# Banded attention: the scores of two heads from 64 rows of the array each, in place of 128 rows with a zero half

## The chip, the cores and the metric

The program runs on one core of a Trainium2 chip. The core has a matrix engine (TensorE, PE in the profile; its weight loads are listed apart as PEld), a vector engine (VectorE, DVE), an activation engine (ScalarE, ACT), a general engine (GpSimd, POOL) and a queue that issues transfers (SyncE, SP). The array of TensorE has 128 rows, one for each partition of its operands, and 128 columns, one for each partition of its result. The metric is the time of one execution in microseconds on the device; the median of several runs counts.

## What is computed

The reference is a stack of layers on 512 tokens of width 1024: one layer pair with feed-forward, mLSTM and windowed attention, then two layers with other mixers. The part that the change touches is the windowed attention: 16 query heads of size 64, 4 key and value heads, each block of 128 queries against the blocks of keys before, at and behind it.

```
def window_attention(x, w_in, sink, w_out):
    p = x @ w_in
    q = p[..., :nq].reshape(B, nb, BLOCK, N_KV_HEADS, GROUP, HEAD_DIM)
...
    s = jnp.einsum('bnqkgd,bnskd->bnkgqs', q, kw).astype(jnp.float32) * (HEAD_DIM ** -0.5)
...
    s = s - slopes[:, :, None, None] * dist
    s = jnp.where(valid[None, :, None, None], s, MASK_VALUE)
    m = jnp.maximum(jnp.max(s, axis=-1, keepdims=True), sink_l)
    pe = jnp.exp(s - m)
    attn = pe / (jnp.sum(pe, axis=-1, keepdims=True) + jnp.exp(sink_l - m))
    o = jnp.einsum('bnkgqs,bnskd->bnqkgd', attn, vw.astype(jnp.float32)).reshape(B, S, nq)
    return o.astype(x.dtype) @ w_out
```

## The kernel before

The program is a row of stages written out by hand for each engine: each stage has one method for each engine, each engine runs its own list of instructions in order, and semaphores, raised by `then_inc` and awaited by `wait_ge`, tie the lists together. Weights come in units of 128 x 1024 (`fetch`), ScalarE rounds a unit to `whi` (L209), VectorE forms the rest `wlo` (L217), and a projection makes three matmuls for each product (L236 to L238, and L349 to L351 in the output projections). Both copies run ahead of TensorE by a fixed number of units (`AHEAD`).

`Window` is the attention stage. Its first part is a projection of 12 units. Units 0 and 1 give the keys, transposed: 128 partitions are two key heads of 64 each. Units 2 and 3 give the values, which TensorE turns (L1097). Units 4 to 11 give the queries, two heads in the 128 partitions of one unit: `self.q[:, x, :]` holds the head that uses the first key head of its pair in partitions 0 to 63, and the one that uses the second in 64 to 127.

The keys lie in `self.kz`, of 128 partitions, two variants `g`, two units and 512 tokens. Variant 0 has the key head of partitions 0 to 63 and zeros below; variant 1 has zeros above and the key head of partitions 64 to 127. ScalarE writes the one half of a unit (L1149), VectorE the other (L1193), and GpSimd writes the zeros (L1243) as soon as the memory of the stage before is free. A score matmul (L1113) takes all 128 partitions of `q` and one variant, and the zeros cancel the other head.

The second part is a loop over 32 blocks, (t, i): the pair of heads t, and in it the four blocks of 128 queries i. Blocks at the ends (i is 0 or 3) see two blocks of keys, 256 columns; the others three, 384 columns. A block goes through these steps:

- scores, PE L1113: two matmuls, one for each head g, into banks 2 (n mod 2) + g;
- bias and maximum, DVE: `ws` (L1212, one for each head), the maximum (L1218), its minimum with the sink (L1220, L1222);
- exponentials, ACT: `wp` (L1166, two, with the sums) and one of the sink (L1168);
- the sum and its reciprocal, DVE (L1227, L1229), and the scaling of `wp`, POOL (L1250);
- transposes, PE L1138: `wp` into banks 4 and 5, and their copy to `wt`, ACT L1182;
- output, PE L1127 (PV in what follows): `wt` with the values; the head g takes columns 64 g to 64 g + 63 of the array;
- behind the fourth block of a pair: `xh` (ACT L1174) and `xl` (DVE L1235), the operand of the output projection.

TensorE's list in turn m is: scores of block m + 1, output of block m - 4, transposes of block m - 3. ScalarE's is: exponentials of block m, `xh` of block m - 4 if it is the fourth, `wt` of block m - 3. DVE's is: bias and maximum of block m, sum and reciprocal of block m - 1, `xl` of block m - 4. A 32-bit matmul appears in the trace as two records, each with its own weight load; a transpose as one. So a block has four records of scores.

Before the first scores TensorE waits for the last queries (`wev`), for DVE's half of the keys (`wkv`), for the values (`wvt`) and for GpSimd's zeros (`wzero`).

Of the kernel before, what the change touches and what calls it, by code (L numbers as in the profile page):

```python
# [7 lines left out]
P = 128  # L8
T = 512
# [1053 lines left out]
class Window:  # L1063
# [4 lines left out]

    def __init__(self, c, u0, before, after, scope):
        self.c, self.u0, self.before, self.after = c, u0, before, after  # L1070

        def sb(name, shape):
            return c.sb("w" + name, shape, F32, scope)

        self.q, self.kz, self.vt = sb("q", [P, 8, T]), sb("k", [P, 2, 2, T]), sb("v", [P, 4, 2 * P])
        self.dist, self.nsink = sb("d", [P, 3 * P]), sb("ns", [P, 16])
        self.sx = [sb(f"s{i}", [P, 2, 3 * P]) for i in range(2)]
        self.pp = [sb(f"p{i}", [P, 2, 3 * P]) for i in range(4)]
        self.pt = [sb(f"t{i}", [P, 2, 3 * P]) for i in range(2)]
        self.small = [sb(f"m{i}", [P, 16]) for i in range(3)]  # L1080
# [5 lines left out]
    def tensor(self, t):  # L1086
# [12 lines left out]
        for p in range(8, 12):  # L1099
            t.wait_ge(*at("wev", p))  # L1100
        t.wait_ge(*at("wkv", 1))
        t.wait_ge(*at("wvt", 1))
        t.wait_ge(*at("wzero", 1))
        n_units = len(self.blocks)
        for m in range(-1, n_units + 4):
            if m + 1 < n_units:
                n = m + 1
                x, i = self.blocks[n]
                j0, j1 = self.near(i)
                if n >= 2:  # L1110
                    t.wait_ge(*at("wbias", n - 2))
                for g in range(2):
                    ins = t.matmul(c.bank(2 * (n % 2) + g)[:, 0:(j1 - j0 + 1) * P], self.q[:, x, i * P:(i + 1) * P],  # L1113
                                   self.kz[:, g, x // 4, j0 * P:(j1 + 1) * P], start=True, stop=True)
                ins.then_inc(*up("wqk", n))
# [25 lines left out]
    def scalar(self, a):  # L1141
        c = self.c
        up, at = c.up, c.at
        for p in range(12):
            c.hi(a, self.u0 + p + AHEAD)
            a.wait_ge(*at("gemm", "unit", self.u0 + p))
            b = c.bank(p % 4)
            if p < 2:
                a.activation(self.kz[0:64, 0, p, :], b[0:64, :], COPY).then_inc(*up("wev", p))  # L1149
            elif p < 4:  # L1150
                a.activation(c.tmp[p % 2], b, COPY).then_inc(*up("wev", p))
            else:
                a.activation(self.q[:, p - 4, :], b, COPY, scale=0.125).then_inc(*up("wev", p))
# [30 lines left out]
    def vector(self, v):  # L1184
# [3 lines left out]
        for p in range(12):  # L1188
            c.lo(v, self.u0 + p + AHEAD)
            if p < 2:  # L1190
                v.wait_ge(*at("gemm", "unit", self.u0 + p))
                v.wait_ge(*at("wev", p))
                v.tensor_copy(self.kz[64:128, 1, p, :], c.bank(p)[64:128, :]).then_inc(*up("wkv", p))  # L1193
            elif p in (5, 6):
                v.wait_ge(*at("wturn", "v", p - 5))
                v.tensor_copy(self.vt[:, :, (p - 5) * P:(p - 4) * P], blocks(c.bank(p - 1))).then_inc(*up("wvt", p - 5))
# [40 lines left out]
    def gpsimd(self, g):  # L1237
        c = self.c
        up, at = c.up, c.at
        g.wait_ge(*at(*self.after))  # L1240
        g.wait_ge(*at(*self.before.pool_end()))
        for k in range(2):
            g.memset(self.kz[64 - 64 * k:128 - 64 * k, k, :, :], 0.0).then_inc(*up("wzero", k))  # L1243
            g.wait_ge(*at("wzero", k))
        for n, (x, i) in enumerate(self.blocks):
# [839 lines left out]
def build(nc, xin, xtin, wst, vec, row, tab, mats_in, out, plan):  # L2085
    with ExitStack() as ctx:
# [5 lines left out]
        for step in plan:  # L2092
# [13 lines left out]
            else:  # L2106
                with ExitStack() as scope:
                    if kind == "mlstm":
                        mixer, ver = Mlstm(c, u, before, scope), "m"
                    elif kind == "window":  # L2110
                        mixer, ver = Window(c, u, before, after, scope), "w"
                    else:
# [216 lines left out]
```

## Time and profile before

| | us |
|---|---|
| median of 3 runs | 3798.38 |
| lowest and highest | 3796.67, 3801.94 |
| the profiled execution | 3797.86 |
| its span, first to last instruction | 3796.0 |
| mean granted clock of TensorE | 0.973 |

Of the span, PE is busy 3587.8 us, DVE 1702.9, ACT 1300.8 and POOL 284.1. The attention loop runs from 1549 to 1647 us of the span. All rows below come from the one profiled execution; times in them are microseconds from the start of its span, mean durations nanoseconds. A matmul's duration includes its passage through the array, so two records that follow each other overlap in the trace, and the distance of their starts is what one costs.

### The profile page before, as it was taken

To read this page: it belongs to the slowest core of one execution; us is meant where nothing else is said; L and a number is where in the kernel's file an instruction comes from. 1 tells how busy PE (TensorE), PEld (TensorE's weight loads), DVE (VectorE), ACT (ScalarE), POOL (GpSimd) and SP (SyncE) were. 2 spreads that over 40 slices of the span, in tenths; PEclk is the share of its full clock that TensorE was granted. 3 is DMA by queue.
4 is the path that set the end of the run, shared out by engine and by line. 5 is a ranking of instruction groups with operands and counts; after the bars stand their busy time and mean duration, and the time that the engine had idled before them with its cause. 6 is when DMAs were issued, how large, how long until landed. Compare 5 with 4: busy or idle time off the path is not lost.

```text
span 3796.0 us, 42550 instructions
## 1 busy us (share of the span) xinstructions
PE 3587.8 (95%) x17294; PEld 2903.9 (76%) x17294; DVE 1702.9 (45%) x2375; ACT 1300.8 (34%) x2112; POOL 284.1 (7%) x342
## 2 busy tenths in 40 slices
PE   8999999899999999989998997899999987899999
PEld 7888756788888888678887875678888875678887
DVE  3334454533343324663334676544333766544332
ACT  3222334322222222532222555333222555333221
POOL 0000001000000001210001121110000221210000
PEclk9999999999999999999999898899999998899999
DMA  4332211233322232112332112002332211003232
GB/s 156 100 100 88 71 34 56 73 100 99 110 81 95 94 117 77 48 45 95 99 100 96 61 62 67 17 28 89 100 100 79 101 59 64 17 28 96 93 105 72
DMA packets 86896, 301.30 MB, mean 79 GB/s; under 512 B 9264, under 2 KB 14128, under 8 KB 86704
## 3 DMA queue, kind: packets, MB, share of 16 engines
q1 hardware_dynamic: 86704, 298.59, 23.8%
q8 instruction: 138, 2.26, 0.3%
q14 instruction: 54, 0.44, 0.0%
HBM read 296.46 MB, written 2.10 MB: 79 GB/s over the span
## 4 chain that ended last, share of the span: by engine, by line
PE 80%; DVE 12%; ACT 4%; issue 3%; POOL 1%; DMA 0%; DVEq 0%; SPq 0%; ACTq 0%; POOLq 0%
PE ps L236 16%; PE ps L237 16%; PE ps L238 16%; PE ps L349 7%; PE ps L350 7%; PE ps L351 7%; PE ps L1947 2%; PE ps L846 1%; PE ps L1919 1%; DVE wlo L217 1%; PE ps L1959 1%; DVE tmp L1812 1%; PE ps L1910 1%; PE ps L1944 1%; DVE rows L1741 1%
## 5 line engine op out<-in xcount | busy, mean ns | idle before, releaser
L236 PE MATMUL ps<-xh,whi 128*128 128x512 f32 (+2 forms) x3128 | 1218.9, 390 | 38.7 <-DVE xl L489 13.0
L237 PE MATMUL ps<-xl,whi 128*128 128x512 f32 (+2 forms) x3128 | 1183.9, 378 | 0.0
L238 PE MATMUL ps<-xh,wlo 128*128 128x512 f32 (+2 forms) x3128 | 1183.3, 378 | 0.0
L217 DVE TENSOR_TENSOR wlo<-raw,whi 128x1024 fp32r<-128x1024 f32 x535 | 660.4, 1256 | 677.2 <-ACT whi L209 676.5
L236 PEld LDWEIGHTS ps<-xh,whi 128*128 128x128 f32 x3128 | 601.2, 192 | 170.9 <-issue 48.8
L209 ACT ACTIVATE whi<-raw 128x1024 fp32r<-128x1024 f32 x535 | 547.7, 1050 | 534.9 <-PE ps L351 527.9
L237 PEld LDWEIGHTS ps<-xl,whi 128*128 128x128 f32 x3128 | 600.9, 192 | 113.9 <-issue 10.6
L238 PEld LDWEIGHTS ps<-xh,wlo 128*128 128x128 f32 x3128 | 600.4, 192 | 108.5
L679 DVE TENSOR_TENSOR tmp<-tmp,ps 128x512 f32<-128x512 f32 x132 | 90.8, 688 | 826.1 <-ACT tmp L664 741.5
L350 PE MATMUL ps<-wlo,hh 128*128 128x512 f32 x1056 | 415.6, 394 | 0.0
L349 PE MATMUL ps<-whi,hh 128*128 128x512 f32 x1056 | 415.3, 393 | 0.0
L351 PE MATMUL ps<-whi,hl 128*128 128x512 f32 x1056 | 410.2, 388 | 0.0
L664 ACT ACTIVATE tmp<-ps 128x512 f32<-128x512 f32 x132 | 78.9, 598 | 901.3 <-PE ps L238 901.3
L349 PEld LDWEIGHTS ps<-whi,hh 128*128 128x128 f32 x1056 | 198.3, 188 | 45.4
L351 PEld LDWEIGHTS ps<-whi,hl 128*128 128x128 f32 x1056 | 198.2, 188 | 44.5
L350 PEld LDWEIGHTS ps<-wlo,hh 128*128 128x128 f32 x1056 | 198.6, 188 | 39.3
L618 POOL TENSOR_SCALAR xr<-xr,st 128x512 f32<-128x512 f32 x18 | 18.8, 1043 | 1575.6 <-DVE xr L463 1575.6
L681 DVE TENSOR_TENSOR hl<-tmp,hh 128x512 fp32r<-128x512 f32 x132 | 91.5, 693 | 92.2 <-ACT hh L666 92.2
L666 ACT ACTIVATE hh<-tmp 128x512 fp32r<-128x512 f32 x132 | 83.5, 632 | 124.1 <-DVE tmp L679 124.1
L349 PE MATMUL ps<-whi,xh 128*128 128x512 f32 x256 | 101.7, 397 | 14.6 <-DVE xl L1038 9.4
L1982 ACT ACTIVATE np<-ps,nsm 128x128 f32<-128x128 f32 (+3 forms) x128 | 66.3, 522 | 118.8 <-DVE nsm L2051 118.8
L350 PE MATMUL ps<-wlo,xh 128*128 128x512 f32 x256 | 100.6, 393 | 0.0
(295 smaller groups left out, 3290.7 us busy)
## 6 DMA issues: line engine op xcount, KB each, us to landing
raw<-in_w SPq DMA_DIRECT2D x535, 512.0 KB, 3.3
rows<-in_row SPq DMA_DIRECT2D x15, 512.0 KB, 4.6
xr<-in_xt SPq DMA_DIRECT2D x2, 1024.0 KB, 7.2
xr<-in_x SPq DMA_DIRECT2D x1, 2048.0 KB, 7.8
ntb<-in_tab SPq DMA_DIRECT2D x2, 832.0 KB, 5.9
htb<-in_tab SPq DMA_DIRECT2D x2, 640.0 KB, 4.1
out<-tmp SPq DMA_DIRECT2D x4, 256.0 KB, 3.0
out<-rows SPq DMA_DIRECT2D x4, 256.0 KB, 2.3
```

Source lines behind the costliest of these rows:

```text
L209: a.activation(self.whi[u % NW][:, :], self.raw[u % NRAW][:, :], COPY).then_inc(*self.up("whi", u))
L217: v.tensor_tensor(self.wlo[u % NW][:, :], self.raw[u % NRAW][:, :], f32(self.whi[u % NW][:, :]), SUB).then_inc(*self.up("wlo", u))
L236: t.matmul(out, wh, xh, start=first, stop=False)
L237: t.matmul(out, wh, xl, start=False, stop=False)
L238: return t.matmul(out, wl, xh, start=False, stop=last)
L349: t.matmul(b, xh[:, k, sl], wh, start=k == 0, stop=False)
L350: t.matmul(b, xh[:, k, sl], wl, start=False, stop=False)
L351: ins = t.matmul(b, xl[:, k, sl], wh, start=False, stop=k == self.k - 1)
L664: a.activation(c.tmp[j % 2], self.bank(j, 0), SILU).then_inc(*c.up("silu", s, j))
L666: a.activation(self.hh[:, j, :], c.tmp[2 + j % 2], COPY).then_inc(*c.up("hh", s, j))
L679: v.tensor_tensor(h, c.tmp[j % 2], self.bank(j, 1), MULT).then_inc(*c.up("gated", s, j))
L681: v.tensor_tensor(self.hl[:, j, :], h, f32(self.hh[:, j, :]), SUB).then_inc(*c.up("hl", s, j))
```

## The change

The variants with zeros go. `self.k` holds the keys of a unit once, two heads in 128 partitions, and ScalarE writes all of it in one copy for each unit. A score matmul takes only the 64 partitions of its head from `q` and from `k`, that is rows 0 to 63 of the array for g = 0 and rows 64 to 127 for g = 1. VectorE's copies, GpSimd's memsets and the waits for both (`wkv`, `wzero`) are gone, as is the argument `after`, which only the memsets used. Banks, columns, order of blocks and all else stay.

```diff
-        self.q, self.kz, self.vt = sb("q", [P, 8, T]), sb("k", [P, 2, 2, T]), sb("v", [P, 4, 2 * P])
+        self.q, self.k, self.vt = sb("q", [P, 8, T]), sb("k", [P, 2, T]), sb("v", [P, 4, 2 * P])
...
-        t.wait_ge(*at("wkv", 1))
         t.wait_ge(*at("wvt", 1))
-        t.wait_ge(*at("wzero", 1))
...
                 for g in range(2):
-                    ins = t.matmul(c.bank(2 * (n % 2) + g)[:, 0:(j1 - j0 + 1) * P], self.q[:, x, i * P:(i + 1) * P],
-                                   self.kz[:, g, x // 4, j0 * P:(j1 + 1) * P], start=True, stop=True)
+                    d = slice(64 * g, 64 * g + 64)
+                    ins = t.matmul(c.bank(2 * (n % 2) + g)[:, 0:(j1 - j0 + 1) * P], self.q[d, x, i * P:(i + 1) * P],
+                                   self.k[d, x // 4, j0 * P:(j1 + 1) * P], start=True, stop=True)
...
             if p < 2:
-                a.activation(self.kz[0:64, 0, p, :], b[0:64, :], COPY).then_inc(*up("wev", p))
+                a.activation(self.k[:, p, :], b, COPY).then_inc(*up("wev", p))
...
-            if p < 2:
-                v.wait_ge(*at("gemm", "unit", self.u0 + p))
-                v.wait_ge(*at("wev", p))
-                v.tensor_copy(self.kz[64:128, 1, p, :], c.bank(p)[64:128, :]).then_inc(*up("wkv", p))
-            elif p in (5, 6):
+            if p in (5, 6):
...
-        g.wait_ge(*at(*self.after))
-        g.wait_ge(*at(*self.before.pool_end()))
-        for k in range(2):
-            g.memset(self.kz[64 - 64 * k:128 - 64 * k, k, :, :], 0.0).then_inc(*up("wzero", k))
-            g.wait_ge(*at("wzero", k))
```

On VectorE the rows of the projection part of the stage stood so before, up to the first bias of the loop (`wk` are the keys, `wv` the values, `wns` the negated sink):

```order
L1187 TENSOR_SCALAR wns<-vc 128x16
L1193 COPY wk<-ps 64x512
L217 TENSOR_TENSOR wlo<-raw,whi 128x1024
L1193 COPY wk<-ps 64x512
L217 TENSOR_TENSOR wlo<-raw,whi 128x1024 x4
L1196 COPY wv<-ps 128x4x128
L217 TENSOR_TENSOR wlo<-raw,whi 128x1024
L1196 COPY wv<-ps 128x4x128
```

and stand so now:

```order
L1186 TENSOR_SCALAR wns<-vc 128x16
L217 TENSOR_TENSOR wlo<-raw,whi 128x1024 x5
L1191 COPY wv<-ps 128x4x128
L217 TENSOR_TENSOR wlo<-raw,whi 128x1024
L1191 COPY wv<-ps 128x4x128
```

Two copies of half a unit of keys are gone between the splits of weights, and nothing else moved. On TensorE the opening of the loop, from the last matmul of the projection on, was before (behind "waits" stand the semaphores of the instruction):

```order
L238 MATMUL ps<-xh,wlo 128x512
L1113 MATMUL ps<-wk,wq 128x256 [waits s_wkv,s_wev,s_wvt,s_wzero]
L1113 MATMUL ps<-wk,wq 128x256
L1113 MATMUL ps<-wk,wq 128x384 x2
L1113 MATMUL ps<-wk,wq 128x384 [waits s_wbias]
L1113 MATMUL ps<-wk,wq 128x384
L1113 MATMUL ps<-wk,wq 128x256 [waits s_wbias]
```

and is now:

```order
L238 MATMUL ps<-xh,wlo 128x512
L1112 MATMUL ps<-wk,wq 128x256 [waits s_wev,s_wvt]
L1112 MATMUL ps<-wk,wq 128x256
L1112 MATMUL ps<-wk,wq 128x384 x2
L1112 MATMUL ps<-wk,wq 128x384 [waits s_wbias]
L1112 MATMUL ps<-wk,wq 128x384
L1112 MATMUL ps<-wk,wq 128x256 [waits s_wbias]
```

The order on TensorE is the same through the whole program; two waits of one instruction are gone, and the score matmuls have half the rows.

## Rows read from the trace of the kernel before

**Rows 1.** The page, part 1: busy us, share of the span, instructions.

```profile
PE 3587.8 (95%) x17294; PEld 2903.9 (76%) x17294; DVE 1702.9 (45%) x2375; ACT 1300.8 (34%) x2112; POOL 284.1 (7%) x342
```

**Rows 2.** Stretches: length, busy PE, PEld, DVE, ACT, POOL, granted clock, DMA, GB/s.

```profile
1549.47:1634.92 85.45, 77.11 (x535) 52.65 (x534) 73.26 (x226) 60.77 (x190) 31.17 (x60) 1.00 0.02 7
1578.93:1590.15 11.22, 10.58 (x78) 7.37 (x77) 9.40 (x31) 8.16 (x26) 4.16 (x8) 1.00 0.01 2
```

**Rows 3.** Waits in 1549.4 to 1634.9: total us, times, longest.

```profile
ACT wp L1166 <- DVE wm L1220: 23.5, 24, 1.9
...
DVE xl L1235 <- ACT xh L1174: 7.8, 6, 1.5
...
PEld ps L1138 <- issue: 4.6, 27, 0.2
...
DVE wlo L217 <- ACT whi L209: 4.2, 1, 4.2
...
ACT wt L1182 <- PE ps L1138: 0.8, 2, 0.4
```

**Rows 4.** Timeline of settled blocks: start, us, instruction, idle before in brackets.

```profile
1575.34 1.03 PE L1113 MATMUL ps<-wk,wq 128*128 128x256 f32 x4
...
1577.13 0.75 DVE L1212 SCALAR_TENSOR_TENSOR ws<-wd,ps 128x256 f32<-128x256 f32 x2
...
1579.93 0.57 ACT L1174 ACTIVATE xh<-ps 128x512 fp32r<-128x512 f32 x1
1580.01 1.46 PE L1113 MATMUL ps<-wk,wq 128*128 128x384 f32 x4
...
1580.53 0.69 DVE L1235 TENSOR_TENSOR xl<-ps,xh 128x512 fp32r<-128x512 f32 x1 [1.26 <-ACT xh L1174]
1581.14 0.74 DVE L1212 SCALAR_TENSOR_TENSOR ws<-wd,ps 128x256 f32<-128x256 f32 x2
```

**Rows 5.** Groups by form in 1547.5 to 1645: busy us, mean ns, idle before.

```profile
L1113 PE MATMUL ps<-wk,wq 128*128 128x384 f32 x64 | 23.5, 490 | 1.0 <-DVE ws L1212 1.0
L1113 PEld LDWEIGHTS ps<-wk,wq 128*128 128x128 f32 x128 | 21.9, 190 | 11.2 <-DVE ws L1212 4.8 <-ACT wq L1153 1.3
...
L1113 PE MATMUL ps<-wk,wq 128*128 128x256 f32 x64 | 16.7, 384 | 2.9 <-DVE ws L1212 1.9 <-ACT wq L1153 0.9
```

**Rows 6.** Timeline: output and transposes of blocks with 384 columns.

```profile
1584.77 1.15 PE L1127 MATMUL ps<-wt,wv 128*64 128x128 f32 x12 [0.61 <-ACT wt L1182]
...
1585.84 0.88 PE L1138 MATMUL ps<-res,wp 128*128 128x128 f32 x6
```

**Rows 7.** Timeline: the opening of the loop.

```profile
1547.67 2.39 PE L1113 MATMUL ps<-wk,wq 128*128 128x256 f32 x8 [0.95 <-ACT wq L1153]
...
1549.47 0.74 DVE L1212 SCALAR_TENSOR_TENSOR ws<-wd,ps 128x256 f32<-128x256 f32 x2
```

**Rows 8.** Timeline: the end of the first period.

```profile
1567.14 0.60 ACT L1182 ACTIVATE wt<-ps 128x512 f32<-128x512 f32 x1 [0.41 <-PE ps L1138]
...
1569.32 0.69 DVE L1235 TENSOR_TENSOR xl<-ps,xh 128x512 fp32r<-128x512 f32 x1 [1.51 <-ACT xh L1174]
```

**Rows 9.** What goes, and beside what: line L1193, a stretch, timelines.

```profile
L1193 DVE COPY wk<-ps x2: 694/694/694, 1489.3 to 1492.0; 64x512 f32<-64x512 f32 x2
...
1487.00:1520.00 33.00, 33.00 (x170) 28.02 (x169) 10.03 (x10) 9.71 (x13) 0.00 (x0) 1.00 0.29 96
...
1469.44 1.95 POOL L1243 MEMSET wk<- 64x1024 f32 x2 [0.51 <-PE ps L351]
...
1469.94 1.27 DVE L485 TENSOR_TENSOR xl<-ps,xh 128x512 fp32r<-128x512 f32 x2
...
1096.81 1.27 DVE L485 TENSOR_TENSOR xl<-ps,xh 128x512 fp32r<-128x512 f32 x2
```

**Rows 10.** Clock: two stretches, as in rows 2, and a timeline row.

```profile
1470.00:1475.00 5.00, 3.64 (x18) 3.67 (x19) 4.54 (x9) 1.04 (x2) 1.33 (x2) 0.67 0.92 311
...
1471.36 0.35 PE L236 MATMUL ps<-xh,whi 128*128 128x256 f32 x1 [1.98 <-DVE xl L485]
...
1640.00:1645.00 5.00, 3.41 (x36) 2.60 (x34) 0.00 (x0) 1.41 (x2) 0.00 (x0) 1.00 0.00 0
```

More of the change, by code:

```diff
@@ L1067, with __init__ @@
     blocks = [(t, i) for t in range(8) for i in range(4)]
-    def __init__(self, c, u0, before, after, scope):
-        self.c, self.u0, self.before, self.after = c, u0, before, after
+    def __init__(self, c, u0, before, scope):
+        self.c, self.u0, self.before = c, u0, before
         def sb(name, shape):
             return c.sb("w" + name, shape, F32, scope)
-        self.q, self.kz, self.vt = sb("q", [P, 8, T]), sb("k", [P, 2, 2, T]), sb("v", [P, 4, 2 * P])
+        self.q, self.k, self.vt = sb("q", [P, 8, T]), sb("k", [P, 2, T]), sb("v", [P, 4, 2 * P])
         self.dist, self.nsink = sb("d", [P, 3 * P]), sb("ns", [P, 16])
@@ L2110, in build @@
                     elif kind == "window":
-                        mixer, ver = Window(c, u, before, after, scope), "w"
+                        mixer, ver = Window(c, u, before, scope), "w"
                     else:
```

## The prediction

> **What bounds the kernel now.** I read the page's busy times first, then the busy times by stretch, the waits of the attention loop, and last the timeline of single blocks. Over the whole program TensorE is busy 95% of the span [rows 1]. That number says little here, because the change touches one stage, the attention loop, and that stage has its own limit. The stretch table shows it. The loop runs from 1549.47 to 1634.92, 85.45 us for 32 blocks. One pass over a pair of heads (four blocks, which I call a period) takes 11.22 us, and in it PE counts 10.58 us busy and DVE 9.40 us [rows 2]. By busy share PE looks like the limit.
>
> The waits say otherwise. In the loop DVE waits for ScalarE's xh, 7.8 us in 6 pieces, and for ScalarE's whi once, and for nothing else: there is no wait of DVE for PE. ScalarE waits 23.5 us for DVE's maximum (L1220) and for PE only twice, 0.8 us in all [rows 3]. So the chain of the loop is bias, maximum, minimum with the sink (DVE), exponentials (ScalarE), once a period the copy to xh (ScalarE), then xl and the next bias (DVE). The timeline shows where the scores stand to it. The pair of score matmuls that starts at 1575.34 has ended by 1576.37, and DVE takes its result at 1577.13, 0.76 us later; at the change of heads ScalarE's xh at 1579.93 releases xl at 1580.53, and the bias follows at 1581.14 without a pause [rows 4]. The scores are always early. In the tail behind 1634.92 there are none, and at the head DVE starts its first bias at 1549.47, when the split of weights ahead of it (L217, which had waited for ScalarE's whi) is through, while the first scores began at 1547.67 [rows 3, 7].
>
> **The change, part by part.**
>
> Score matmuls, L1113: 32 pairs, four records each. A pair with 384 columns lasts 1.46 us from the first start to the last end, the mean record 0.490, so the records start (1.46 - 0.49) / 3 = 0.32 us apart; with 256 columns the pair lasts 1.03 and the record 0.384, so 0.215 apart [rows 4, 5]. A record is not made cheaper by having fewer rows; what can shrink is the distance, since the two heads now sit in different rows of the array and write different banks. In program order the records are A1 A2 B1 B2. The least gain is that nothing overlaps (four distances, as now). The most is that the pair costs two distances. I take three, A2 beside B1, because the nearest row points between: PV (L1127), whose two heads already take different columns, has 12 records in 1.15 us, 0.096 each, where the transposes, which use all columns, have 6 in 0.88, 0.147 each [rows 6]. Three distances free 16 x 0.32 + 16 x 0.215 = 8.6 us of PE over the loop; two would free 17.1 us. **None of this is on the path in a settled period**: PE then waits longer for ScalarE's wt (it already waits 0.61 us before the PV at 1584.77 [rows 6]), and wt stands in ScalarE's queue behind exponentials that wait for DVE. After the scores come early, DVE is next late, and it is late already.
>
> In one place PE was late. In the first period PE had a backlog, ScalarE waited for its transposes (0.41 us at 1567.14), and DVE's xl at 1569.32 waited 1.51 us, where in a settled period it waits 1.26 [rows 4, 8]. The backlog holds one pair of 384 columns, whose saving of 0.32 us covers it. **Gain: 1.51 - 1.26 = 0.25 us, taken as 0.2.** Bounds: 0 and 0.25, since beyond it DVE's own chain is next.
>
> The mode of the array: today the order is scores (full), PV (half the columns), transposes (full), scores (full), so there are two switches a block; from now on transposes to scores is a third. What a switch costs is seen between PV and transposes: PEld stands 4.6 us in 27 pieces on "issue", 0.17 us each [rows 3]. So 32 x 0.17 = 5.4 us of PE time are added, less than the 8.6 freed. On the path this is between 0 and 5.4 us; I take 0, since the new switch lies ahead of the scores, which have 0.76 us of cover [rows 4], and PE's total falls all the same. The Trainium skill, "TensorEngine Tiling (Array Packing)", Key Properties, states that changing the tiling mode drains the engine; the trace's 0.17 us agrees, and the sum by that rule would be at worst the 5.4 us above.
>
> DVE: two copies of 64 x 512, 0.694 us each, at 1489.3 and 1492.0, go [rows 9]. In that stretch PE is busy 33.00 of 33 us and DVE 10.03 [rows 9]: nothing waited for them. ScalarE's two copies now write 128 rows instead of 64, in the same stretch, where ScalarE is busy 9.71 of 33 us. Both taken as 0; without PE's cover the two copies of DVE would be worth their 1.39 us.
>
> GpSimd: two memsets, 1.95 us together, at 1469.44, go. Its next work is in the loop, and DVE's xl beside them took 1.27 us, exactly as at 1096.81, in the passage between the two plain layers, where no memset runs [rows 9]. So they cost nothing by contention either: 0.
>
> Waits: PE's first score matmul loses two of its four semaphores (wkv, wzero). Both were long set. It may start some tens of ns sooner, and is covered: the first two pairs are issued together from 1547.67 to 1550.06 and DVE wants the first at 1549.47 [rows 7]. 0. No wait is added and no DMA changes. The 4 KB per partition that come free shift addresses and nothing else.
>
> Sum: -0.2 us. The profiled execution took 3797.86 us, 1.86 over its span of 3796.0, and stands 0.5 below the median of 3798.38. From 3798.38 the forecast is **3798.2 us**.
>
> **The rivals.**
>
> 1. The pair does not overlap at all, so that the change does not do what it says. Then PE gains nothing and pays the new switches, behind cover: 3798.4. In favour: A1 A2 B1 B2 is a bad order for overlap. The time can't tell this from the forecast.
>
> 2. The switches reach the path. PE, ScalarE and PE again (wt, PV, transposes, wt) go round nearly as tightly as DVE does, so 0.17 us a block may surface now and then: up to +5.4, 3799 to 3803.8.
>
> 3. Faster: PE is the true bound, as its 10.58 of 11.22 us suggests [rows 2]. Then all that is freed counts: 3798.4 - 8.6 = 3789.8, or 3781.3 with two distances. Against it: no wait of DVE for PE in the loop [rows 3].
>
> 4. Slower, in the loads of weights. Each score record has a load of 0.190 us [rows 5], today hidden beside the record before. If loads into half the rows are not hidden, a period has 16 of them, +3.0 us. PE's work in a period is 11.22 - 0.61 = 10.6; it becomes the bound from 0.6 us more, and 13.6 is 2.4 over: x 85.45 / 11.22 = 7.6 periods gives +18, **3817**. Against it: PV's loads into half the columns are hidden (12 records in 1.15 us [rows 6]).
>
> 5. Slower, by the clock. The granted clock was 0.67 on average in 1470 to 1475, where PE had just stood still for 1.98 us [rows 10]; of its two levels, 1.2 and 2.4 GHz, it was at the lower for most of that stretch. The change makes PE idler: before PV and in the opening of the loop its waits grow by a few tenths. Were the clock at 1.2 GHz for the whole loop, PE's work of 10.6 us a period, less the 2 x 0.32 + 2 x 0.215 = 1.07 freed, 9.5, would be 19.1, +7.8 x 7.6 = +60, 3858; a single stretch of 5 us at that level costs at most 2.5. It decides once the low level holds for more than three such stretches. Against it: in 1640 to 1645, with PV and transposes alone and PE busy 3.41 of 5 us, the granted clock is 1.00 [rows 10], and the loop will stay busier than that. The Trainium skill, "TensorE: Matmul & The Clock Gate", Part 4: PE-mode transpose, states that transposes don't count as activity in the same way; that would leave scores and PV alone to hold the clock, with the price just given. The same row speaks against it.
>
> **Chances.** Forecast 0.60; no overlap 0.17; switches partly on the path 0.08. These three are within 0.2% (7.6 us, about what a measurement of this kernel can tell from no change): 0.85. Faster, rival 3: 0.05. Slower: rival 4 0.05, rival 5 0.05, together 0.10. The range is that of the three equal cases with the spread of the runs shown (3796.67 to 3801.94), one stretch of low clock more or less (2.5 us) and the 5.4 us of switches: 3794.0 to 3804.0. It leaves out rivals 3 to 5, 0.15.
>
> **What the profile after would show.** A score pair of 384 columns, 1.46 us now, should last 0.64 + 0.49 = 1.13 us (0.81 with two distances, 1.46 with no overlap), and one of 256 columns 0.81 instead of 1.03. PE's wait for ScalarE's wt should grow. The period should stay 11.22 us, with xl waiting 1.26 us in all periods, the first one too; DVE should still have no wait for PE. A line "DVE <- PE" in the loop, score loads that no longer lie beside matmuls, or a granted clock under 1.00 between 1550 and 1635 would make the prediction wrong; so would a period under 11.2 us, which would mean that PE was in the chain after all.

## The result and the profile after

The changed kernel takes 3805.12 us, median of 20 runs (3791.99 to 3808.82), against 3797.55 us for the kernel before on the same chip (20 runs, 3792.56 to 3801.94). The ratio of the mean times, here as everywhere below, is 1.0018, with a 95% interval of 1.0011 to 1.0024: slower, by about 0.2%, where no change was forecast, and the median is 1.1 us outside the range. The profiled execution took 3803.18 us, with a span of 3801.3, against 3797.86 and 3796.0.

The page of the changed kernel, the span and part 1, against [rows 1]:

```profile
span 3801.3 us, 42541 instructions
...
PE 3584.8 (94%) x17294; PEld 2896.5 (76%) x17294; DVE 1701.2 (45%) x2373; ACT 1301.2 (34%) x2112; POOL 282.5 (7%) x340
```

TensorE is busy 3 us less and the span is 5.3 us longer. So the totals say nothing again. Next comes the timeline of settled blocks of the changed kernel (the columns are as in [rows 4]; PEld rows are loads of weights):

```profile
1619.94 0.30 PEld L1112 LDWEIGHTS ps<-wk,wq 64*128 64x128 f32 x4 [0.17 <-issue]
1619.94 0.70 PE L1112 MATMUL ps<-wk,wq 64*128 64x256 f32 x4
...
1624.43 0.57 ACT L1173 ACTIVATE xh<-ps 128x512 fp32r<-128x512 f32 x1
...
1624.51 0.92 PE L1112 MATMUL ps<-wk,wq 64*128 64x384 f32 x4
1625.04 0.69 DVE L1230 TENSOR_TENSOR xl<-ps,xh 128x512 fp32r<-128x512 f32 x1 [1.27 <-ACT xh L1173]
...
1629.27 0.93 PE L1126 MATMUL ps<-wt,wv 128*64 128x128 f32 x10 [1.42 <-ACT wt L1181]
```

The change does what it says. A pair of 384 columns lasts 0.92 us where it lasted 1.46, and one of 256 columns 0.70 where it lasted 1.03 [rows 4, 5]. The four loads lie beside each other (0.30 us in all), and the new switch ahead of them is the 0.17 us on "issue". And as forecast, the saved time is turned into waiting: TensorE stands 1.42 us for wt before an output of 384 columns, where it stood 0.61 [rows 6], while xl waits 1.27 us as before.

The windows of the changed kernel show where the time goes (columns as in [rows 2]: length, busy time of the engines, granted clock, DMA):

```profile
1547.50:1550.00 2.50, 1.42 (x4) 0.51 (x4) 2.40 (x7) 0.93 (x4) 0.00 (x0) 0.68 0.46 126
1550.00:1560.00 10.00, 7.25 (x30) 3.77 (x29) 9.41 (x31) 6.32 (x25) 4.17 (x8) 0.50 0.06 23
1560.00:1562.50 2.50, 2.50 (x12) 1.15 (x11) 1.56 (x6) 1.73 (x4) 0.94 (x2) 0.59 0.00 0
1578.93:1590.15 11.22, 9.37 (x81) 5.96 (x76) 9.39 (x30) 8.17 (x27) 4.18 (x8) 1.00 0.01 2
1549.47:1634.92 85.45, 70.73 (x539) 43.97 (x536) 72.02 (x224) 60.87 (x190) 31.30 (x60) 0.93 0.02 6
1636.25:1649.41 13.16, 9.49 (x56) 7.10 (x56) 0.92 (x4) 3.30 (x6) 0.94 (x2) 0.61 0.01 1
1650.00:1660.00 10.00, 9.54 (x35) 7.77 (x36) 2.35 (x3) 1.38 (x2) 0.00 (x0) 0.83 0.16 52
```

The third column from the end is the granted clock. A settled period still takes 11.22 us with DVE 9.39 busy, the very numbers of before. But the clock, 1.00 from 1500 to 1696 us before, is at 0.50, the lower of its two levels (1.2 of 2.4 GHz), in all of 1550 to 1560, and again for most of the tail and for a part of the output projection behind it. The trace's record of the granted clock dates these low stretches: 13.7 us from 1548.4, 10.2 us from 1637.2, 3.4 us from 1650.8. The kernel before has none of the three. The runs without a timeline fit this, since each has its mean granted clock on record: 0.969 to 0.971 in 19 of the 20 runs of the changed kernel, and 0.974 in the one that took 3791.99 us; 0.973 or 0.974 in all 35 runs of the kernel before that stand beside the first experiments.

What the low clock does is to be seen in the timeline and in the waits of 1540 to 1650, again of the changed kernel:

```profile
1562.31 1.02 DVE L1207 SCALAR_TENSOR_TENSOR ws<-wd,ps 128x384 f32<-128x384 f32 x2 [0.84 <-PE ps L1112]
...
1639.90 2.03 PE L1126 MATMUL ps<-wt,wv 128*64 128x128 f32 x12 [0.90 <-ACT wt L1181]
1641.86 1.54 PE L1137 MATMUL ps<-res,wp 128*128 128x128 f32 x6
```

```profile
DVE xl L1230 <- ACT xh L1173: 21.8, 8, 12.2
PE ps L1126 <- ACT wt L1181: 15.5, 19, 1.4
ACT wt L1181 <- PE ps L1137: 12.1, 6, 3.6
...
DVE ws L1207 <- PE ps L1112: 0.8, 1, 0.8
```

An output of 12 records takes 2.03 us in place of 1.15, six transposes 1.54 in place of 0.88 [rows 6]. In the tail, where nothing is left for DVE, ScalarE waits up to 3.6 us for the transposes, and the last xl waits 12.2 us, where it waited 8.5. And the line "DVE <- PE", which the prediction named as the mark of its own failure, is there: once, 0.8 us, under the low clock.

To place the loss over the whole program I matched ScalarE's activations of the two traces one by one (both have 1766) and subtracted their times. The table gives that difference in us for several kernels, each time against the trace of before; its columns are places in the program, by the time of before. It is worked out from the traces and is no view of the profile.

```
                372    412   1560   1620   1664   1701   2050   2146   3789
after          -0.8   -1.4   -1.7   -0.4   +4.9   +5.0   +5.0   +5.0   +5.3
changed_again  -0.4   -1.0   -1.1   +0.3   +5.5   +4.2   +4.9   +4.9   +5.8
rows_only      -0.4   -1.0   -1.3   +0.1   +2.5   +2.5   +2.5   +2.5   +2.1
rest_only      +0.4   +0.4   +0.3   +0.3   +0.3   +0.3   +0.3   +0.3   +0.5
same_rows      +0.6   +0.6   -1.5   +4.1   +4.1   +2.8   +3.5   +3.5   +4.7
half_cols      +0.8   +0.8   +1.0   +2.3   +3.9   +2.5   +3.3   +3.3   +4.9
fill           +0.4   +0.4   +0.5   +1.6   +1.5   +1.5   +1.5   +3.1   +4.2
fill_half      -0.7   -1.2   -1.5   -0.4   +1.2   -0.1   +0.6   -8.4   -8.1
fill_open      -0.1   -0.7   -1.1   -0.1   +1.6   +0.2   +1.0   -8.0   -7.9
fill_tail      +0.1   +0.1   +0.1   +1.5   +3.1   +1.7   +2.5   +2.4   +3.8
next_before    +0.2   +0.3   +0.1    0.0    0.0    0.0    0.0   -8.9   -6.7
next_after     -0.1    0.0   -0.1   +1.3   +6.5   +5.1   +5.8   -3.1   -3.3
next_fill      -0.1    0.0   -0.2   +0.4   +0.3   +0.3   +0.3   -8.5   -6.6
```

The changed kernel comes into the attention 1.7 us ahead of before, which has nothing to do with the change (0.8 at the start of the program, 0.6 at a low stretch near 379 that this execution did not have, and the rest in small pieces). From 1560 to 1664 it loses 6.6 us: 1.3 in the opening, and 5.3 in the tail with the first part of the output projection. Behind that only 0.4 us are lost until the end.

### The profile page after: what moved, and what is told of

Its sections match the earlier page's. It is cut to its first block, busy times and chain, and to the rows that moved or that the text cites. A ratio compares the mean times of both kernels' runs of the same rounds, so it can differ in the third digit from the quotient of the medians.

```text
span 3801.3 us, 42541 instructions
## 1 busy us (share of the span) xinstructions
PE 3584.8 (94%) x17294; PEld 2896.5 (76%) x17294; DVE 1701.2 (45%) x2373; ACT 1301.2 (34%) x2112; POOL 282.5 (7%) x340
## 4 chain that ended last, share of the span: by engine, by line
PE 80%; DVE 12%; ACT 4%; issue 3%; POOL 1%; DMA 0%; DVEq 0%; SPq 0%; ACTq 0%; POOLq 0%
PE ps L236 16%; PE ps L238 16%; PE ps L237 16%; PE ps L350 7%; PE ps L349 7%; PE ps L351 7%; PE ps L1937 2%; PE ps L846 1%; PE ps L1909 1%; DVE wlo L217 1%; PE ps L1949 1%; DVE tmp L1802 1%; PE ps L1900 1%; PE ps L1934 1%; DVE xr L435 1%
## 5 line engine op out<-in xcount | busy, mean ns | idle before, releaser
L351 PE MATMUL ps<-whi,xl 128*128 128x512 f32 x256 | 101.2, 395 | 0.0
```

The lines of the kernel that those rows point to most:

```text
L351: ins = t.matmul(b, xl[:, k, sl], wh, start=False, stop=k == self.k - 1)
```

## Experiments

Each kernel is compared with runs of the kernel before on the same chip, whose median was 3797.08 or 3797.11 us each time; n is the number of its own runs. A timeline is one execution of each kernel.

**Which part of the change it is.** rows_only is the kernel before with the one line of the score matmuls changed; the zeros, copies, memsets and waits all stay:

```diff
-                    ins = t.matmul(c.bank(2 * (n % 2) + g)[:, 0:(j1 - j0 + 1) * P], self.q[:, x, i * P:(i + 1) * P],
-                                   self.kz[:, g, x // 4, j0 * P:(j1 + 1) * P], start=True, stop=True)
+                    d = slice(64 * g, 64 * g + 64)
+                    ins = t.matmul(c.bank(2 * (n % 2) + g)[:, 0:(j1 - j0 + 1) * P], self.q[d, x, i * P:(i + 1) * P],
+                                   self.kz[d, g, x // 4, j0 * P:(j1 + 1) * P], start=True, stop=True)
```

> The kernel before with the score matmuls alone changed: they take 64 rows of q and the half of kz that is not zero; memsets, the copies of VectorE and the four waits stay. Theory I (idle): the score pairs take half of TensorE's time, TensorE idles more where the loop opens and where it ends, and the granted clock falls there; then this kernel shows it all: ratio to before about 1.002 (1.001 to 1.0025), clock under 1.00 in the opening (1548 to 1562) and in the tail (1636 to 1655). Theory II (rows): the clock falls because matmuls of 64 rows count for less, overlap or not: the same here. Theory III (the rest): copies, memsets, waits and moved addresses make the difference: ratio 1.000 here, clock 1.00 in both places.

Measured: 3805.11 us (n = 12), ratio 1.0017 [1.0008, 1.0025].

rest_only is the reverse, the changed kernel with 128 rows for its score matmuls (its keys hold no zeros, so it sums the scores of the two heads):

```diff
-                    d = slice(64 * g, 64 * g + 64)
-                    ins = t.matmul(c.bank(2 * (n % 2) + g)[:, 0:(j1 - j0 + 1) * P], self.q[d, x, i * P:(i + 1) * P],
-                                   self.k[d, x // 4, j0 * P:(j1 + 1) * P], start=True, stop=True)
+                    ins = t.matmul(c.bank(2 * (n % 2) + g)[:, 0:(j1 - j0 + 1) * P], self.q[:, x, i * P:(i + 1) * P],
+                                   self.k[:, x // 4, j0 * P:(j1 + 1) * P], start=True, stop=True)
```

> The changed kernel with the score matmuls back at 128 rows, on the keys without zeros, so each score sums two heads (the product of the other head is not masked; the work of TensorE is that of before). Theories I and II: ratio 1.000 (0.9995 to 1.0005), score pairs of 1.46 and 1.03 us, clock 1.00 in the opening and the tail. Theory III: ratio about 1.002, clock falls as in the changed kernel.

Measured: 3797.62 us (n = 11), ratio 1.0000 [0.9992, 1.0009]. The stretch 1550 to 1560 and the tail, of rows_only and then of rest_only:

```profile
1550.00:1560.00 10.00, 7.25 (x30) 3.34 (x27) 9.44 (x31) 6.67 (x26) 3.80 (x8) 0.50 0.09 35
1640.00:1650.00 10.00, 6.29 (x44) 4.90 (x45) 1.20 (x2) 3.28 (x5) 0.00 (x0) 0.78 0.00 0
```

```profile
1550.00:1560.00 10.00, 6.08 (x21) 3.21 (x20) 9.45 (x29) 5.61 (x21) 3.17 (x6) 1.00 0.16 53
1640.00:1650.00 10.00, 6.68 (x53) 5.21 (x52) 1.92 (x2) 2.95 (x4) 0.00 (x0) 1.00 0.05 10
```

What follows: the score matmuls alone make the loss, by the times of the runs. The profiled execution of rows_only, 3800.00 us, is one of its faster ones: it has the 13.7 us at half clock in the opening, but only 6.8 in the tail, and loses 3.7 us from 1560 to 1664 where the changed kernel loses 6.6. How far the tail falls is thus not the same in each execution. The copies, memsets and waits that went are worth nothing, as forecast, and so are the shifted addresses.

**Is it idleness, or the rows?** TensorE works less on the scores and at fewer rows; two kernels separate these. same_rows puts both heads of a pair into rows 0 to 63 (head 2 of each pair is not computed), so that they can't overlap and TensorE works as long as before. half_cols keeps all 128 rows and halves the columns (half of the scores is not computed):

```diff
-                    d = slice(64 * g, 64 * g + 64)
+                    d = slice(0, 64)
```

> The changed kernel with both score matmuls of a pair in rows 0 to 63 (head 0 computed twice, the second head left out): half the rows, but nothing can overlap, so a pair of 384 columns should take about 1.46 us again, not 0.92. Theory I: TensorE is as busy as before, clock 1.00 in the opening and tail, ratio 1.000 (at most 1.0005). Theory II: half the rows count for less, clock falls, ratio 1.001 to 1.0025.

Measured: 3806.98 us (n = 11), ratio 1.0019 [1.0011, 1.0028].

```diff
-                    d = slice(64 * g, 64 * g + 64)
-                    ins = t.matmul(c.bank(2 * (n % 2) + g)[:, 0:(j1 - j0 + 1) * P], self.q[d, x, i * P:(i + 1) * P],
-                                   self.k[d, x // 4, j0 * P:(j1 + 1) * P], start=True, stop=True)
+                    w = (j1 - j0 + 1) * P // 2
+                    ins = t.matmul(c.bank(2 * (n % 2) + g)[:, 0:w], self.q[:, x, i * P:(i + 1) * P],
+                                   self.k[:, x // 4, j0 * P:j0 * P + w], start=True, stop=True)
```

> The changed kernel with score matmuls of all 128 rows but half the columns (half of each block's scores left out and the heads summed): TensorE's time for a pair is that of the changed kernel (about 0.9 us for the long pairs) with full rows. Theory I: the clock falls in the opening and the tail, ratio 1.001 to 1.0025. Theory II: full rows hold the clock, ratio 1.000.

Measured: 3799.40 us (n = 11, 3790.58 to 3802.73), ratio 0.9998 [0.9989, 1.0007]; its runs stand in two groups, five from 3790.6 to 3792.5 with a mean clock of 0.974 or 0.975, and six from 3799.4 to 3802.7 with 0.971 or 0.972, so the median means little. Pair of 384 columns in the settled part, same_rows, then half_cols:

```profile
1606.87 1.55 PE L1112 MATMUL ps<-wk,wq 64*128 64x384 f32 x4
```

```profile
1604.61 0.82 PE L1112 MATMUL ps<-wk,wq 128*128 128x192 f32 x4
```

The stretch 1550 to 1560 of same_rows, and of half_cols:

```profile
1550.00:1560.00 10.00, 8.56 (x25) 4.59 (x24) 9.12 (x30) 6.48 (x26) 4.07 (x8) 0.56 0.08 30
```

```profile
1550.00:1560.00 10.00, 6.60 (x20) 4.89 (x20) 9.48 (x29) 5.48 (x19) 2.40 (x5) 0.56 0.15 53
```

The pair of 384 columns just ahead of the fall, in same_rows, and the same pair in rest_only, where nothing falls:

```profile
1548.75 1.55 PE L1112 MATMUL ps<-wk,wq 64*128 64x384 f32 x4 [0.28 <-DVE ws L1207]
```

```profile
1550.54 1.56 PE L1111 MATMUL ps<-wk,wq 128*128 128x384 f32 x4 [0.28 <-DVE ws L1206]
```

What follows: the plain form of "TensorE is idler, so the clock falls" does not hold. In same_rows TensorE's work and pauses are those of rest_only to 0.1 us until the clock falls, and it falls for 17.1 us from 1551.3, longer than in the changed kernel. Nine of its eleven runs have a mean clock of 0.969 to 0.972, rest_only's all 0.973 or 0.974. Its settled part is denser too (a pair takes 1.55 us against 1.46), and holds 1.00. The opening costs it 5.6 us in the table against 1.3, since its pairs don't overlap and TensorE at half clock is the bound (DVE waits for its scores three times, 5.0 us in all). But half_cols falls as well, for 13.7 us from 1551.3, with all rows in use and less time at work. So in this opening neither all the rows nor the full time at work was enough alone; what decides these runs don't tell. Nor do the two profiles show the larger part of the loss, that of the tail: from 1636 to 1650 the clock is 1.00 in both, and half_cols has only 3.4 us at half clock behind it. The slower runs of same_rows, 3806 to 3808 us at 0.969 or 0.970, may have more; none of them has a timeline.

**Does the clock carry the loss?** If so, extra work for TensorE that nobody reads has to make the kernel faster. The opening is where TensorE has room: of 1550 to 1560 the kernel before fills 6.04 us. fill adds one 128-row matmul of 512 columns behind the scores of blocks 1 to 4, into a bank that is free there, and one of 384 columns behind the transposes of each of the last four blocks, the first of them behind a wait for the last bias, so that its bank is free; fill_half has the same with 64 rows; fill_open and fill_tail have one of the two places alone:

```diff
+        def fill(n, w):
+            t.matmul(c.bank(n)[:, 0:w], self.q[:, 0, 0:P], self.q[:, 1, 0:w], start=True, stop=True)
...
                 ins.then_inc(*up("wqk", n))
+                if 1 <= n <= 4:
+                    fill(4, 512)
...
                 ins.then_inc(*up("wturn", n))
+                if n == n_units - 4:
+                    t.wait_ge(*at("wbias", n_units - 1))
+                if n >= n_units - 4:
+                    fill(0, 384)
```

> The changed kernel with extra matmuls, whose result is written and never read, that use all 128 rows of the array: one of 512 columns behind the scores of each of blocks 1 to 4 in the opening of the attention, and one of 384 columns behind the transposes of each of its last four blocks. Theory R (rows at work hold the clock; half the rows for the scores lets it fall): both fallen stretches, of 13.7 us from 1548.4 and of 10.2 and 3.4 us from 1637.2, were gone or at least much shorter, and the 5.3 to 7 us that they cost come back. By the shared runs of rest_only (3797.6 us), which has the scores at full rows and otherwise the same code, the ratio would be 0.999 to 1.0002. Theory W (the time is lost in the work itself, by TensorE taking longer for the pair or its new switches, and the clock is only a by-product of the execution): the fillers add work of TensorE, 4 x (0.43 or more) and 4 x (0.32 or more) us at the rate of the settled blocks' 384-column scores (1.46 us for a pair of two at full rows), so the ratio stays at 1.0018 or rises to 1.0025. Theory C (the clock falls by the chip's state, whatever stands in the attention): as the changed kernel, 1.0018.

Measured: 3795.57 us (n = 11, 3789.85 to 3802.18), ratio 0.9996 [0.9987, 1.0005].

> As the run before it, but the extra matmuls use rows 0 to 63 of the array alone: the same time at work of TensorE, half the rows. Theory R: they do less or nothing for the clock, so the low stretches stay, the ratio is 1.0015 to 1.0025, and it differs from that of the kernel with full-row fillers by 0.001 or more. A theory of time at work alone (the clock looks at how long TensorE is busy): the low stretches go as with full rows and the ratio is 0.999 to 1.0002.

Measured: 3791.87 us (n = 11), ratio 0.9991 [0.9982, 1.0000].

> The changed kernel with the four full-row fillers of the opening alone. If the account of the profiled pair is right, the opening lost 1.3 us and the tail with the output projection 5.7: the low stretch at 1548 goes and that near 1637 stays, and the ratio is 1.0010 to 1.0016. If the opening carries most of the loss: 1.0005 or less.

Measured: 3790.17 us (n = 10; eight of them from 3789.2 to 3791.1, the others 3795.1 and 3802.6), ratio 0.9985 [0.9976, 0.9994].

> The changed kernel with the four full-row fillers of the last four blocks alone. By the same account the low stretches from 1637 to 1655 go and that of the opening stays: ratio 1.0000 to 1.0006. If the opening carries most of the loss: 1.0012 or more.

Measured: 3800.70 us (n = 10), ratio 1.0009 [1.0000, 1.0018].

The stretch 1550 to 1560 of fill, fill_half, fill_open and fill_tail, in this order:

```profile
1550.00:1560.00 10.00, 7.33 (x28) 2.60 (x26) 9.45 (x30) 5.49 (x22) 2.98 (x6) 1.00 0.16 53
```

```profile
1550.00:1560.00 10.00, 6.83 (x35) 3.58 (x34) 9.45 (x30) 6.51 (x26) 4.04 (x8) 0.94 0.07 27
```

```profile
1550.00:1560.00 10.00, 7.30 (x36) 3.42 (x34) 9.41 (x32) 6.61 (x25) 3.66 (x7) 0.96 0.11 42
```

```profile
1550.00:1560.00 10.00, 6.90 (x22) 2.83 (x24) 9.45 (x28) 5.65 (x21) 3.22 (x6) 0.52 0.15 52
```

What follows: the fillers of the opening lift the clock in the opening, and those of the tail don't lift it there. With them one low stretch of 3.4 us is left there, which begins at 1558.9 to 1561.0; without them it lasts 13.7. In the tail, fill has no low stretch at all; fill_open and fill_half have 3.4 us near 1648, fill_tail 3.4 from 1649.4, all of them less than the 10.2 and 3.4 of the changed kernel. So most of the tail comes right by itself once the opening does: fill_open, whose tail has the very code of the changed kernel, loses 1.6 us from 1620 to 1664 where that loses 5.3. The tail's fillers do as much by themselves: fill_tail leaves the opening as it is and loses 1.6 as well. Why the tail falls at all, when its work is the same in both, stays open. fill_half does not bear out the expectation that half rows do nothing: as extra work on top they do about what full rows do. That is against a rule by rows alone, as half_cols was.

Three more expectations did not come out. By the account of the profile fill_open was to be at 1.0010 or more, and it is faster than before; 1.0005 or less was named for an opening that carries most of the loss, which its profile doesn't show. fill_tail, at 1.0009, lies between its two branches. half_cols has the ratio of full rows that hold the clock, and a clock that falls. And fill, which has the cleaner attention, is slower than fill_open. The table shows why. fill_open leaves the attention 1.6 us behind before (2.7 lost on the way), and then gains 9.0 us between 2050 and 2146, in another stage, in which no code differs. The window 2090 to 2110 of before, and of fill_open:

```profile
2090.00:2100.00 10.00, 8.69 (x48) 8.69 (x48) 5.59 (x26) 4.78 (x11) 0.00 (x0) 0.64 0.15 52
2100.00:2110.00 10.00, 10.00 (x48) 10.00 (x48) 1.22 (x1) 2.83 (x3) 0.00 (x0) 0.50 0.07 13
```

```profile
2090.00:2100.00 10.00, 7.81 (x70) 7.74 (x70) 6.53 (x30) 5.73 (x15) 0.00 (x0) 1.00 0.17 54
2100.00:2110.00 10.00, 10.00 (x60) 8.78 (x60) 6.21 (x8) 8.65 (x12) 0.23 (x1) 1.00 0.32 105
```

Before has a low stretch of 20.5 us from 2092.9, in dense work of TensorE, and fill_open has none. It is a second place where the clock decides, and it comes and goes between executions. The groups of times fit it: between the two groups of half_cols the mean clock differs by about 0.003, which over 3800 us is some 20 us more or less at half clock (an estimate, from rounded clocks). As long as it does so, a small difference in the attention is read through it.

**The second place held still.** Just ahead of it TensorE of the kernel before waits 2.51 us for VectorE's xl:

```profile
2091.31 0.33 PE L236 MATMUL ps<-xh,whi 128*128 128x128 f32 x1 [2.51 <-DVE xl L489]
```

I filled this wait, in the kernel before (next_before) and in the changed one (next_after), and in a third kernel (next_fill) together with fillers behind the scores of blocks 1 to 6 in the opening of the attention (those behind 5 and 6 into bank 7). changed_again is the changed kernel once more.

```diff
                 self.turn_t(t, 2 + m, h)
+        if self.then is not None:
+            for _ in range(16):
+                t.matmul(banks[1][:, 2 * P:], c.w(u0, 0)[0], c.xh[:, 0, 0:2 * P], start=True, stop=True)
         for i in (2, 3):
```

> The kernel before with 16 extra matmuls of 256 columns (about 0.12 us each, result never read) in one wait of the stage behind the attention: ahead of the first 128-column matmuls of its projection, where TensorE waits 2.51 us at 2091.31 for xl, and behind which the profiled run of before shows the low clock for 20.5 us from 2093. The attention is untouched. Theory P (that stretch is the clock's answer to the 2.51 us wait, and worth 8 to 9 us wherever it comes): low stretch gone, 1.00 from 2090 to 2120, ratio 0.9975 to 0.9980 in nearly all executions, as in the two profiled runs in which it was absent (offsets of 9.0 us between 2090 and 2160). Theory Q (that stretch depends on something else): ratio 1.000.

Measured: 3790.55 us (n = 11, 3788.74 to 3791.91), ratio 0.9982 [0.9973, 0.9991].

> The changed kernel with the same 16 extra matmuls in the stage behind the attention and nothing else. Against before: if the loss of the change is made within the attention and its output projection alone, the median is that of the run before it plus 5 to 8 us (ratio 0.9990 to 1.0000); if half or more of the 7.6 us between the medians of before and after came from how often the later stretch falls, it is within 3 us of it (0.9975 to 0.9985).

Measured: 3793.43 us (n = 11, 3789.28 to 3796.42), ratio 0.9988 [0.9979, 0.9997].

> The changed kernel with those 16 matmuls and with six full-row fillers in the opening of the attention (behind the scores of blocks 1 to 6 in place of 1 to 4). Theory R (clock): the attention's opening costs nothing or at most the 1.1 us of the earlier run, the low stretch at 2093 is gone, and the median is 3786 to 3790 us, ratio 0.9970 to 0.9980, faster than both kernels and at or below the kernel before with the same 16 matmuls. If extra matmuls cost what they save: at or above that kernel.

Measured: 3790.94 us (n = 11, 3788.92 to 3792.64), ratio 0.9983 [0.9974, 0.9992].

> The changed kernel once more, for a second profile. If the low stretches belong to the change and not to the one execution, they stand again in the opening (from about 1548, some 14 us) and near the end of the attention (from about 1637, 3 to 10 us), and the time lies in 3799 to 3809 us; how many of those at 379, 1690 and 2133 stand with them differs by the execution.

Measured: 3803.71 us, one run; low stretches of 13.7 us from 1549.2, 10.2 from 1637.9 and 3.4 from 1651.6.

The filled wait and the two windows in next_before:

```profile
2088.63 2.15 PE L426 MATMUL ps<-xh,whi 128*128 128x256 f32 x16
2091.38 0.33 PE L236 MATMUL ps<-xh,whi 128*128 128x128 f32 x1 [0.60 <-DVE xl L492]
```

```profile
2090.00:2100.00 10.00, 9.40 (x84) 9.20 (x83) 5.65 (x27) 5.18 (x13) 0.00 (x0) 1.00 0.16 54
2100.00:2110.00 10.00, 10.00 (x56) 8.67 (x56) 6.58 (x8) 9.21 (x14) 1.10 (x1) 1.00 0.32 105
```

The attention of next_after and of next_fill:

```profile
1550.00:1560.00 10.00, 7.12 (x24) 3.05 (x26) 9.39 (x29) 5.65 (x21) 3.24 (x6) 0.51 0.16 52
...
1640.00:1650.00 10.00, 7.51 (x45) 5.65 (x43) 0.00 (x0) 2.22 (x3) 0.00 (x0) 0.54 0.00 0
```

```profile
1550.00:1560.00 10.00, 8.29 (x35) 3.28 (x36) 9.38 (x30) 5.71 (x22) 3.23 (x6) 1.00 0.16 52
1560.00:1570.00 10.00, 9.68 (x76) 5.87 (x72) 7.51 (x25) 7.90 (x25) 4.17 (x8) 1.00 0.01 2
...
1640.00:1650.00 10.00, 6.68 (x53) 5.25 (x53) 1.91 (x2) 2.95 (x4) 0.00 (x0) 1.00 0.05 9
```

What follows. First, sixteen matmuls that compute nothing make the kernel before 6.5 us faster, and all its runs now lie within 3.2 us; in the profiled execution 9.0 us are won at the place, of which 1.5 go again at a low stretch from 2140.8 and 0.8 further on. The length of the wait alone does not decide. In fill_open it is unfilled, and the clock stays at 1.00 from 2090 to 2120:

```profile
2092.26 0.33 PE L236 MATMUL ps<-xh,whi 128*128 128x128 f32 x1 [2.19 <-DVE xl L489]
```

In fill it is 1.65 us long, and 23.9 us at half clock follow.

Second, the loss from 1560 to 1664 is the same 6.6 us in all three profiles of the changed attention without fillers (after, changed_again, next_after), and 3.7 in rows_only. So it comes back with the change, but not in full each time: three of the 32 runs of after and rows_only, 3791.99, 3792.45 and 3795.40 us, have a mean clock of 0.974, as the kernel before has; whether the attention or a later stage held the clock in them, no timeline tells. Third, with the second place held still, the medians of the two kernels lie 2.9 us apart and not 7.6. The profiles say how: next_after loses 6.6 in the attention, but has no low stretch at 1697 and none at 2140.8, where next_before has both; it gets back 0.6 by the first and 1.5 by the second, and 1.1 more against that kernel between 2200 and 2350, so that 3.3 us are left at the end. Fourth, with fillers in the opening the clock is 1.00 through the whole attention, the tail included, where nothing was added, the loss falls from 6.6 us to 0.5 (the table, -0.2 to +0.3), and the median is 0.4 us over that of next_before. The 0.5 is lost right behind 1560, where the fillers behind blocks 5 and 6 stand directly ahead of transposes and outputs: the likely price of too many of them, which no run takes apart. A kernel that beats both was therefore found, but not by this change: next_before has it with the old scores, and the changed attention adds nothing to it. The forecasts of the three were somewhat too good: 0.9982 for next_before and 0.9983 for next_fill lie just over their ranges, and next_fill was to be at or below next_before. next_after, 2.9 us over next_before, fits the branch that puts half or more of the 7.6 us on the later stretch.

## Why the prediction was wrong

**The chain of the loop: right.** The period is 11.20 to 11.24 us in every profile, xl waits 1.26 to 1.27 us in the settled part, and the freed time of TensorE went into its wait for wt. Rival 3, TensorE as the true bound, is dead: it would have shortened the period, where TensorE is now busy 9.37 us in place of 10.58.

**The size of the overlap: somewhat off, harmless.** Three distances were taken, 1.13 us for a pair of 384 columns; two would have been 0.81. Measured are 0.92, nearer to two; with 256 columns 0.70, midway between 0.60 and 0.81. The Trainium skill, "TensorEngine Tiling (Array Packing)", Theoretical Speedup, gives up to 2x for a dimension of 64 or less; this trace shows 1.46 / 0.92 = 1.6 on the whole pair.

**Switches, copies, memsets, waits: right at 0.** rest_only, at 1.0000, bears out all but the switches. The switches are there, 0.17 us each, and a period of 11.22 us has no room for them on the path. Rival 4 is out: the loads are hidden.

**The gain of 0.2 us in the first period: not seen.** There the changed kernel is at half clock. No run has the changed opening at full clock without fillers, so it stays untested.

**The clock: here it failed.** The prediction put the clock at nothing in its sum, and that is the step that failed: 13.7 us at half clock in the opening cost 1.3 us, and 13.6 us in the tail and the projection behind it 5.3. Rival 5 was the right mechanism, with a chance of 0.05. These of its steps were wrong.

- Its case rested on one row, 1640 to 1645, where a TensorE busy for 3.41 of 5 us held the clock [rows 10]. Under the changed kernel 1640 to 1650, with the same transposes and outputs, is at 0.54 to 0.63 (next_after, changed_again and after). That the scores ahead of it use half the rows is not the whole reason: fill_open and next_fill have such scores too, and are at 1.00 in 1640 to 1645. One row at the higher level shows what held there, and nothing of how near to the edge it was.
- "The loop will stay busier than that" was reasoned from a settled period. The clock did stay at 1.00 in all settled periods. It fell in the opening, the idlest part, which the prediction had looked at for another question [rows 7] and never asked about the clock. The window and the timeline of the kernel before, which should have been read there, and then the first pair of the changed kernel beside them:

```profile
1550.00:1560.00 10.00, 6.04 (x24) 3.39 (x25) 9.41 (x29) 5.65 (x21) 3.22 (x6) 1.00 0.17 52
```

```profile
1550.27 1.56 PE L1113 MATMUL ps<-wk,wq 128*128 128x384 f32 x4 [0.21 <-DVE ws L1212]
1552.31 1.13 PE L1113 MATMUL ps<-wk,wq 128*128 128x256 f32 x4 [0.48 <-DVE ws L1212]
1554.89 1.13 PE L1113 MATMUL ps<-wk,wq 128*128 128x256 f32 x4 [1.45 <-DVE ws L1212]
```

```profile
1548.58 1.65 PE L1112 MATMUL ps<-wk,wq 64*128 64x384 f32 x4 [1.31 <-DVE ws L1207]
```

  TensorE works 6.04 of 10 us there before the change, with scores as its only work for most of it. The shorter pairs turned the pause of 0.21 us into one of 1.31, and the low stretch begins in it. Rival 5 had these waits grow "by a few tenths"; that is about what one pair saves, but two are issued together there, and they shrank from 2.39 us to 1.35.
- Busy time was taken as the measure. same_rows, with the busy time of before up to the fall and half the rows, loses the clock as well. The chance that half-used rows go with another clock was not on the list.

The price was nearly right: "a single stretch of 5 us costs at most 2.5"; 3.4 us of low clock in the dense output projection cost 1.6 (half_cols, table, 1620 to 1664), and in the opening 13.7 us cost only 1.3, since DVE's chain covers most. The point from which it decides was not wrong either: "more than three such stretches" are over 15 us, and there were 27.3, which cost 6.6 us, most of it in the tail, which has no DVE chain to hide behind. What failed was the case against their coming at all.

**The range.** It allowed one stretch more or less. Its upper end does not hold the terms that it names: 3798.2 and the 5.4 us of switches and the 2.5 of a stretch would be 3806.1, over the 3805.12 measured, so 3804.0 is too narrow by its own sum. The wider range would have held the result by luck, through the switches, which came out at 0. It was also missing that a shift of some us in the attention goes with another clock in a later stage: of the 7.6 us between the medians 2.9 are left once the later wait is filled. The profiles show low stretches that come and go near 379, near 1697, from 2093 and from 2140.8 on; how often each stands in the runs without a timeline stays open.

## What to carry to other kernels

Before shortening work on TensorE that is off the critical path, look for the idlest part of the stage and of what follows it, and ask what the granted clock would cost there; the settled loop doesn't answer that. Half the rows at the same busy time lost the clock here (same_rows), so a busy share that stays is no proof that the clock will. And where the clock record shows a low stretch in dense work behind a wait of some us, work that nobody reads, put into the wait, is a cheap test: here it was worth 6.5 us, nearly the 7.6 between the two kernels that were to be explained.

## What was not expected of the hardware

- Two matmuls in different halves of the rows, writing different banks, overlap for the most part, though the program issues both records of one head before those of the other: 1.46 to 0.92 us with 384 columns, 1.03 to 0.70 with 256. Both in the same half: 1.55.
- The granted clock fell with TensorE's busy time kept, when only rows 0 to 63 worked on the scores (same_rows, 17.1 us at 0.50), and also with all rows and half the columns (half_cols, 13.7 us).
- One wait of 2.51 us on TensorE went with a low clock for 20.5 us in dense work behind it, worth 9.0 us in the trace; filled to 0.60 us, it was gone. But it was gone in fill_open too, with a wait of 2.19 us.
- The low stretches are not tied to the program's start: the one of the opening starts 0.65 us behind the first bias in the changed kernel (1548.4 against 1547.78). In same_rows, with the same code ahead of it, it starts only at 1551.3. The Trainium skill, "TensorE: Matmul & The Clock Gate", Part 1, states that the monitor's window is free-running and does not reset when a kernel starts. The two places of the fall are compatible with it; no run here shows it.
